# Two-layer transformer kernel: where the conformer convolution and its layer norm stand in the second block

## The chip, the cores and the metric

One core of a Trainium2 chip (trn2) runs the whole kernel in one launch. The metric is device time in microseconds (us) of one execution, lower is better. The core has TensorE (PE in the profile; its weight loads are PEld), VectorE (DVE), ScalarE (ACT), GpSimd (POOL), and SyncE (SP), which here issues every DMA.

## The reference

A first block (`first_block`: a gated short convolution, a latent attention, a retention) gives `x`, 512 tokens by 1024. It isn't touched by the change. The second block follows, and all is f32:

```python
def conformer_conv(a, b, dw_w, dw_b, ln_g, ln_b):
    u = a * jax.nn.sigmoid(b)
    ...
    u = lax.conv_general_dilated(u, dw_w[:, None, :], window_strides=(1,), ...,   # 31 taps, depthwise
                                 feature_group_count=C) + dw_b
    u = layer_norm(u, ln_g, ln_b)
    return jax.nn.silu(u)

def second_block(x, ...):
    h = rms_norm_2(x, norm1_g)
    z = jnp.einsum('bsd,dc->bsc', h, w_in)
    q, k = rope(rms_norm_2(heads(z[q]), ...)), rope(rms_norm_2(heads(z[k]), ...))   # 8 heads of 64
    attn = ...                     # three dilated windows, mixed by their log-sum-exp
    conv = conformer_conv(z[a], z[b], ...)                                          # 512 channels
    x = x + jnp.einsum('bsc,cd->bsd', jnp.concatenate([attn, conv]), w_out)
    x = x + expert_choice_moe(rms_norm_2(x, norm2_g), w_router, w1, w3, w2)         # 16 experts, 64 tokens each
```

(`...` and `z[...]` shorten it.) The experts' weights are 16 times 33.8 MB.

## The kernel before

The engines are programmed by hand, each with its own instruction stream in program order; named semaphores tie them together. A wait blocks all that stands behind it on the same engine. `PS[:, b, :]` are the 8 banks of the accumulator memory (PSUM), 128 x 512 f32 each.

The part of the second block that matters here runs in these stages. Feature-major means that channels lie on partitions and the 512 tokens on columns; token-major is the other way round.

1. **Gated input** (`f2_psum`): four groups j of 128 channels of a and b, feature-major, are projected; sigmoid and product give `CU2` (`cu_done`). SyncE then copies `CU2` into shifted copies `RG` (`spread(b)`, 16 DMAs for each b, semaphore `rg_in[b]`), from which the convolution of 128 channels is 32 matmuls in the program (64 in the trace) with the diagonal weights `DWD[b]` that GpSimd builds (`dwd_ready`).
2. **q/k/v loop**, i = 0 to 11: TensorE projects tile t = i % 4 of 128 tokens for q (i < 4), k (i < 8) and v into bank 4 + i % 4 (`z_psum`). For q and k ScalarE squares it and takes a seed of the root (Ln, Exp), VectorE reduces, refines, scales and rotates (`zr_ready`), and TensorE transposes the result in `turn_z(i - 1)`, one projection later. `conv(b)` stands behind projections 1, 3, 5 and 7. ScalarE moves its result to `CA[:, b, :]` (`conv_out`, `cv_done`).
3. **Second attention**, n = 0 to 15 (token tile n // 4, pair of heads n % 4): TensorE makes two score matmuls (`scores2`), VectorE masks them and finds the row maxima (`row_max2`), ScalarE exponentiates (`probs2`), VectorE divides (`norm_p2`), TensorE transposes the 2 x 4 blocks (`turn_p2`), ScalarE copies them out (`pt2_out`), TensorE multiplies by v (`values2`), and after each token tile ScalarE copies the outputs (`yt2_out`, `yt2_evac`).
4. **Layer norm over channels**, spread over the pairs n = 0 to 7 of stage 3 (`LN_AT = 0`): the mean by four matmuls with `LN_ONES` (n = 0), four subtractions on VectorE (`cen_done`) and four squares on ScalarE (`lsq_done`, n = 1), the variance by four matmuls (n = 2), the inverse root (ScalarE's Ln and Exp, then three passes on VectorE), for each group j a scaling and an affine pass (`ly_ready`, n = 3 to 6), ScalarE's Exp(-y) (`ly_exp`), and VectorE's `silu`: add 1, reciprocal, multiply (`y2_done`, n = 4 to 7).
5. **Output projection** `out_project2` with the router between its parts, then top-k on VectorE, then the experts. The expert weights go through a ring of 12 slots of 1.4 MB. SyncE issues the first ten loads once `yt2_evac` is 4 and `y2_done` is 4, two more when the output projection is through, and each later one when TensorE has used the slot (`ring_used`).

What sets the order around the change is thus code order on each engine. SyncE's queue around stage 2 holds, in this order: `spread(0)`, `spread(1)`, the weights of k (group 11, needed at i = 4), `spread(2)`, `spread(3)`, the weights of v (group 12, released by `z_psum` 4), then those of the output projection (13 and 14, released by `z_psum` 8 and 12), then the expert loads.

Of the kernel before, what the change touches and what calls it, by code (L numbers as in the profile page):

```python
# [28 lines left out]
ALU = mybir.AluOpType  # L29
# [109 lines left out]
def build(nc, x, meta, wd, w_uq, w_ukv, w_router, w1, w3, w2, prm, ident_d, tab_d, iota_d, mask_d, out):  # L139
    with ExitStack() as ctx:  # L140
# [146 lines left out]
        pt_evac ptm_evac ps_ready pv_psum yo_free op_psum xo_done ustat2 u2_ready ut2_psum ut2_ready  # L287
        pads dwd_ready conv_psum f2_psum b_exp cu_done z_psum z_sq z_ms z_rs z_free zr_ready zT_psum zT_evac v_evac s2_psum nm2_ready
        p2_done pt2_psum pt2_evA pv2_psum ps2_ready yt2_evac cv_done mean_psum cen_done lsq_done
        var_psum lv_ready lrs_done ly_ready ly_exp y2_done op2_psum xo2_done rstat h2n_ready h2T_psum h2T_ready lg_psum  # L290
# [113 lines left out]
        def _(gp):  # L404
# [35 lines left out]
            for b in range(4):  # L440
                if b == 2:
                    gp.wait_ge(s["ut2_psum"], NT)
# [5 lines left out]
        def _(act):  # L448
# [137 lines left out]
            for t in range(NT):  # L586
                act.wait_ge(s["xo_done"], 2 * t + 2)
                if t >= 2:
                    act.wait_ge(s["ut2_psum"], t - 1)
                own(act.activation(U2[t % 2], X[:, t, :], ACT.Square, accum_out=stat[:, t:t + 1]))  # L590
                own.settle()
                rsqrt_seed(rstd[:, t:t + 1], stat[:, t:t + 1], 1.0 / D).then_inc(s["ustat2"], 1)
# [20 lines left out]
            for i in range(2 * NT):  # L613
# [32 lines left out]
            for n in range(NT * 4):  # L646
# [5 lines left out]
                if n == LN_AT + 1:  # L652
                    for j in range(4):
                        act.wait_ge(s["cen_done"], j + 1)
                        act.activation(LSQ[:, j, :], CA[:, j, :], ACT.Square).then_inc(s["lsq_done"], 1)
                if n == LN_AT + 2:
                    act.wait_ge(s["lv_ready"], 1)
                    own(act.activation(LY, LV, ACT.Ln))
                    own.settle()
                    act.activation(LY, LY, ACT.Exp, scale=-0.5).then_inc(s["lrs_done"], 1)  # L660
                if n >= LN_AT + 3 and n < LN_AT + 7:
                    j = n - LN_AT - 3
                    act.wait_ge(s["ly_ready"], j + 1)
                    if j >= 2:
                        act.wait_ge(s["y2_done"], j - 1)
                    act.activation(SCB[j % 2], CA[:, j, :], ACT.Exp, scale=-1.0).then_inc(s["ly_exp"], 1)
# [4 lines left out]
            for t in range(NT):  # L671
# [3 lines left out]
                rsqrt_seed(rstd[:, t:t + 1], stat[:, t:t + 1], 1.0 / D).then_inc(s["rstat"], 1)  # L675
# [31 lines left out]
        def _(dve):  # L707
# [283 lines left out]
            def norm_row(t):  # L991
                dve.wait_ge(s["ustat2"], t + 1)
                refine(rstd[:, t:t + 1], stat[:, t:t + 1], 1.0 / D)
                dve.tensor_scalar(U2[t % 2], X[:, t, :], rstd[:, t:t + 1], None, ALU.mult).then_inc(s["u2_ready"], 1)

            def rowT_out(t):
                c = t * P
                dve.wait_ge(s["ut2_psum"], t + 1)
# [4 lines left out]
                i.then_inc(s["ut2_ready"], 1)  # L1003
# [10 lines left out]
            for j in range(4):  # L1014
                dve.wait_ge(s["b_exp"], j + 1)
                dve.wait_ge(s["f2_psum"], 2 * j + 2)
                silu(SCB[j % 2], PS[:, (2 * j + 1) % 4, :], CU2[:, j, PAD:PAD + S]).then_inc(s["cu_done"], 1)

            for i in range(2 * NT):
# [21 lines left out]
                dve.tensor_tensor(t1, t1, t2, ALU.add).then_inc(s["zr_ready"], 1)  # L1041

# [22 lines left out]
            for n in range(NT * 4):  # L1065
# [784 lines left out]
```

## Time and profile before

| | |
|---|---|
| median of 3 runs | 2061.91 us (2059.35 to 2061.99) |
| the profiled execution | 2061.4 us, its span 2059.6 us |
| TensorE busy | 1828.9 us, 89% of the span |
| VectorE, ScalarE busy | 477.2 us (23%), 206.9 us (10%) |
| DMA queue q1 | 70.3% of 16 engines' span, 597.93 MB |
| chain that ended last | DMA 48%, PE 39%, SPq 5%, DVE 4%, ACT 2% |

The busy shares are means over stages with different limits, so they don't tell what one stage is worth. The chain tells which work the end waited for at each moment. An idle time on an engine is named with what ended it. The time outside of the span (2061.4 - 2059.6 = 1.8 us) is no part of any view.

### The profile page before, as it was taken

To read this page: it belongs to the slowest core of one execution; us is meant where nothing else is said; L and a number is where in the kernel's file an instruction comes from. 1 tells how busy PE (TensorE), PEld (TensorE's weight loads), DVE (VectorE), ACT (ScalarE), POOL (GpSimd) and SP (SyncE) were. 2 spreads that over 40 slices of the span, in tenths; PEclk is the share of its full clock that TensorE was granted. 3 is DMA by queue.
4 is the path that set the end of the run, shared out by engine and by line. 5 is a ranking of instruction groups with operands and counts; after the bars stand their busy time and mean duration, and the time that the engine had idled before them with its cause. 6 is when DMAs were issued, how large, how long until landed. Compare 5 with 4: busy or idle time off the path is not lost.

```text
span 2059.6 us, 20333 instructions
## 1 busy us (share of the span) xinstructions
PE 1828.9 (89%) x8256; PEld 771.3 (37%) x8256; DVE 477.2 (23%) x965; ACT 206.9 (10%) x413; POOL 15.0 (1%) x30
## 2 busy tenths in 40 slices
PE   7998999989997969998888988988988889889887
PEld 4544446444344533333332332332323323323222
DVE  2453336224328240120110101201201111012011
ACT  2131014000124210000000000000000000000000
POOL 0000000100000000000000000000000000000000
PEclk9899799999997989999999999999999999999999
DMA  6102020034210617999999999999999999999998
GB/s 239 47 0 82 0 82 1 24 116 110 82 42 1 263 75 329 424 424 426 425 426 425 426 426 426 425 426 426 426 426 426 426 425 426 426 426 426 426 425 347
DMA packets 82035, 598.53 MB, mean 291 GB/s; under 512 B 8824, under 2 KB 18168, under 8 KB 32712
## 3 DMA queue, kind: packets, MB, share of 16 engines
q1 hardware_dynamic: 81992, 597.93, 70.3%
q8 instruction: 30, 0.49, 0.1%
q14 instruction: 13, 0.11, 0.0%
HBM read 591.38 MB, written 2.10 MB: 288 GB/s over the span
## 4 chain that ended last, share of the span: by engine, by line
DMA 48%; PE 39%; SPq 5%; DVE 4%; ACT 2%; issue 1%; DVEq 0%; ACTq 0%
DMA arena<-in_w 48%; PE PS L1217 19%; PE PS L1687 5%; SPq L391 5%; PE PS L1601 3%; PE PS L1720 2%; PE PS L1517 1%; PE PS L1340 1%; PE PS L1400 1%; DVE arena L789 1%; PE PS L1270 1%; PE PS L1657 1%; PE PS L1430 1%; PE PS L1414 1%; PE PS L1562 1%
## 5 line engine op out<-in xcount | busy, mean ns | idle before, releaser
L1687 PE MATMUL PS<-arena 128*64 128x512 f32 (+1 forms) x3072 | 639.7, 562 | 112.5 <-DMA arena<-in_w 111.7
L1687 PEld LDWEIGHTS PS<-arena 128*64 128x64 f32 x3072 | 207.6, 136 | 544.9 <-issue 354.8
L1217 PE MATMUL PS<-arena 128*128 128x512 f32 (+6 forms) x1040 | 391.4, 535 | 3.2 <-DVE arena L1000 1.4
L1720 PE MATMUL PS<-arena 128*64 128x512 f32 x1408 | 324.5, 599 | 23.5 <-ACT arena L698 13.1
L1217 PEld LDWEIGHTS PS<-arena 128*128 128x128 f32 (+1 forms) x1040 | 186.0, 194 | 197.5 <-issue 188.6
L1720 PEld LDWEIGHTS PS<-arena 128*64 128x64 f32 x1408 | 115.5, 137 | 222.5 <-issue 168.1
L1182 DVE TENSOR_TENSOR arena<-arena,PS 128x1408 f32<-128x1408 f32 x16 | 25.9, 1621 | 699.0 <-PE PS L1687 699.0
L694 ACT ACTIVATE arena<-PS 128x1408 f32<-128x1408 f32 x16 | 21.5, 1344 | 742.7 <-PE PS L1687 742.7
L1191 DVE COPY arena<-PS 128x512 f32<-128x512 f32 x16 | 11.1, 692 | 328.3 <-PE PS L1720 328.3
L1734 PE MATMUL PS<-arena 64*128 64x512 f32 x256 | 76.7, 626 | 8.9 <-DVE arena L1176 8.1
L1199 DVE TENSOR_TENSOR arena<-arena,PS 128x512 f32<-128x512 f32 x128 | 78.0, 682 | 20.4 <-PE PS L1734 20.4
L1657 PE MATMUL PS<-arena 128*64 128x512 f32 x256 | 59.4, 607 | 1.5 <-DVE arena L1163 1.5
L1601 PE MATMUL PS<-arena 128*128 128x512 f32 x128 | 57.3, 595 | 0.7 <-ACT arena L643 0.7
L789 DVE RECIPROCAL arena<-arena 128x512 f32<-128x512 f32 x16 | 53.6, 3353 | 0.6
L688 ACT ACTIVATE arena<-PS 128x512 f32<-128x512 f32 x16 | 9.6, 598 | 438.6 <-PE PS L1657 438.6
L1734 PEld LDWEIGHTS PS<-arena 64*128 64x128 f32 x256 | 31.1, 185 | 43.4 <-DVE arena L1199 26.0
L1562 PE MATMUL PS<-arena 128*64 128x128 f32 x256 | 19.8, 303 | 16.2 <-ACT arena L639 13.5
L1601 PEld LDWEIGHTS PS<-arena 128*128 128x128 f32 x128 | 23.3, 190 | 26.0 <-issue 25.1
L1657 PEld LDWEIGHTS PS<-arena 128*64 128x64 f32 x256 | 18.8, 140 | 35.5 <-issue 35.5
L787 DVE TENSOR_SCALAR arena<-arena 128x512 f32<-128x512 f32 x16 | 6.8, 426 | 97.6 <-PE PS L1217 44.5
L1707 PEld LDWEIGHTS PS<-arena 128*128 128x128 f32 x176 | 23.0, 213 | 14.6 <-issue 12.2
L1517 PE MATMUL PS<-arena 128*32 128x512 f32 x256 | 28.3, 594 | 0.0
(242 smaller groups left out, 974.3 us busy)
## 6 DMA issues: line engine op xcount, KB each, us to landing
arena<-in_w SPq DMA_DIRECT2D x384, 1408.0 KB, 34.6
arena<-in_w_in SPq DMA_DIRECT2D x5, 2048.0 KB, 7.8
arena<-in_w_in SPq DMA_DIRECT2D x8, 1024.0 KB, 6.4
arena<-in_w_out SPq DMA_DIRECT2D x4, 2048.0 KB, 8.4
arena<-arena SPq DMA_DIRECT2D x64, 67.5 KB, 2.3
arena<-in_tab SPq DMA_DIRECT2D x1, 2304.0 KB
arena<-in_w_in SPq DMA_DIRECT2D x1, 2176.0 KB, 19.2
arena<-in_x SPq DMA_DIRECT2D x4, 512.0 KB, 6.6
```

Source lines behind the costliest of these rows:

```text
L391: sp.dma_start(RING[n % SLOTS], chunk(e, n)).then_inc(ring_in[n % SLOTS], 16)
L789: own(dve.reciprocal(e, e))
L1182: dve.tensor_tensor(HH, S1, PF[:, 3 * 512:3 * 512 + FH], ALU.mult).then_inc(s["hh_done"], 1)
L1199: dve.tensor_tensor(xs, xs, PS[:, [3, 4, 5, 7][n % 4], :], ALU.add).then_inc(s["sc_add"], 1)
L1217: i = pe.matmul(dst, lhs(k), rhs(k), start=k == 0, stop=k == KD - 1)
L1517: ins = pe.matmul(PS[CG_W * i:CG_W * (i + 1), 2 + b % 2, :], DWD[b][:, n * CG_W:(n + 1) * CG_W], RG[4 * b + i][:, SH * q:SH * q + S], star ...
L1562: ins = pe.matmul(PS[64 * f:64 * f + 64, 6, j * P:(j + 1) * P], V2[:, b * 512 + h * HD:b * 512 + (h + 1) * HD], PT2[:, f, b * P:(b + 1) * ...
L1601: ins = pe.matmul(PS[:, i % 4, :], YT2[:, k, t * P:(t + 1) * P], wg[:, k, :], start=k == 0, stop=k == KD - 1)
L1657: i = pe.matmul(PS[64 * f:64 * f + 64, 7, :], SEL[:, t, :], H2N[:, t, f * 512:(f + 1) * 512], start=t == 0, stop=t == NT - 1, skip_group_c ...
L1687: i = pe.matmul(PS[64 * f:64 * f + 64, bank + c // 512, 0:w], XE[:, k, :], slot[:, f * FH + c:f * FH + c + w], start=k == 0, stop=k == KD ...
L1720: ins = pe.matmul(PS[64 * d:64 * d + 64, 6, :], HT[:, j, 64 * f:64 * f + 64], W2R[:, f, j, d * 512:(d + 1) * 512], start=f == 0 and j == 0 ...
L1734: pe.matmul(PS[:, [3, 4, 5, 7][n % 4], :], G[64 * d:64 * d + 64, t * P:(t + 1) * P], YE[64 * d:64 * d + 64, :], start=True, stop=True).the ...
```

## The change

The computation stays. `conv(b)` stands behind projections 0, 1, 2 and 3. The mean's matmuls stand behind projection 4 and use bank 2 in place of bank 7, the variance's behind projection 5 in bank 3. The rest of the layer norm follows on ScalarE and VectorE in the q/k iterations 4 to 6 and behind iteration 7. The sigmoid in it is taken in another way: in place of VectorE's add, reciprocal and multiply, VectorE adds 1 (and caps at 1e18), ScalarE takes Ln and Exp(-x), VectorE multiplies. Stage 3 keeps nothing but the attention. Some semaphores are merged into others with an offset (`ut2_psum` into `ut_psum` from 5 on, and the like), at the same points of the program.

```diff
 ACT, q/k loop
-                if i >= 3 and i % 2 == 1:
-                    conv_out((i - 3) // 2)
-            zT_out(2 * NT - 1)
-            conv_out(3)
-            for t in range(NT):
+                if i < 4:
+                    conv_out(i)
+                if i == 4:
+                    for j in range(4):
+                        act.wait_ge(s["cen_done"], j + 1)
+                        act.activation(LSQ[:, j, :], CA[:, j, :], ACT.Square).then_inc(s["lsq_done"], 1)
+                if i == 5:
+                    act.wait_ge(s["lv_ready"], 1)
+                    own(act.activation(LY, LV, ACT.Ln))
+                    own.settle()
+                    act.activation(LY, LY, ACT.Exp, scale=-0.5).then_inc(s["lrs_done"], 1)
+
+            def ln_exp(j):
+                act.wait_ge(s["ly_ready"], j + 1)
+                if j >= 2:
+                    act.wait_ge(s["y2_done"], j - 1)
+                act.activation(SCB[j % 2], CA[:, j, :], ACT.Exp, scale=-1.0).then_inc(s["ly_exp"], 1)
+
+            def ln_sig(j):
+                act.wait_ge(s["ly_one"], j + 1)
+                own(act.activation(SCB[j % 2], SCB[j % 2], ACT.Ln))
+                own.settle()
+                act.activation(SCB[j % 2], SCB[j % 2], ACT.Exp, scale=-1.0).then_inc(s["ly_sig"], 1)
+            ln_exp(0), ln_exp(1), ln_sig(0), ln_sig(1)
+            zT_out(2 * NT - 1)
+            ln_exp(2), v_out(0), ln_exp(3), ln_sig(2), ln_sig(3)
+            for t in range(1, NT):
+                v_out(t)
 DVE, behind the rotation of q/k iteration i
+                if i == 4:
+                    dve.wait_ge(s["mean_psum"], 1)
+                    dve.wait_ge(s["cv_done"], 4)
+                    for j in range(4):
+                        dve.tensor_tensor(CA[:, j, :], CA[:, j, :], PS[:, 2, :], ALU.subtract).then_inc(s["cen_done"], 1)
+                if i == 5:
+                    dve.wait_ge(s["var_psum"], 1)
+                    dve.tensor_scalar(LV, PS[:, 3, :], EPS, None, ALU.add).then_inc(s["lv_ready"], 1)
+                if i == 6:
+                    dve.wait_ge(s["lrs_done"], 1)
...
+                    ln_affine(0), ln_affine(1)
+            ln_one(0), ln_affine(2), ln_one(1), ln_out(0), ln_affine(3), ln_out(1)
+            ln_one(2), ln_one(3), ln_out(2), ln_out(3)
 DVE, second attention: the same passes and silu leave pairs 1 to 7
-                if LN_AT + 4 <= n < LN_AT + 8:
-                    j = n - LN_AT - 4
-                    dve.wait_ge(s["ly_exp"], j + 1)
-                    silu(SCB[j % 2], CA[:, j, :], YT2[:, 4 + j, :]).then_inc(s["y2_done"], 1)
 PE, q/k loop
-                if i < 2 * NT and i % 2 == 1:
-                    conv(i // 2)
+                if i < 4:
+                    conv(i)
+                if i == 4:
+                    pe.wait_ge(s["cv_done"], 4)
+                    for j in range(4):
+                        ins = pe.matmul(PS[:, 2, :], LN_ONES, CA[:, j, :], start=j == 0, stop=j == 3)
+                    ins.then_inc(s["mean_psum"], 1)
+                if i == 5:
+                    pe.wait_ge(s["cen_done"], 4)
+                    pe.wait_ge(s["lsq_done"], 4)
+                    for j in range(4):
+                        ins = pe.matmul(PS[:, 3, :], LN_ONES, LSQ[:, j, :], start=j == 0, stop=j == 3)
+                    ins.then_inc(s["var_psum"], 1)
```

`ln_affine(j)` is the scaling by LY and the affine pass of group j, `ln_one(j)` the cap and add, `ln_out(j)` the last multiply. The order of the instructions on TensorE in the q/k/v loop before (L1217 is a projection of 8 matmuls, its x80 is the gated input's 64 and projections 0 and 1; L1503 is `turn_z`, L1517 a convolution):

```order
L1217 MATMUL PS<-arena 128x512 x80
L1503 MATMUL PS<-arena 128x128 x4
L1517 MATMUL PS<-arena 32x512 x32
L1217 MATMUL PS<-arena 128x512 x8
L1503 MATMUL PS<-arena 128x128 x4
L1217 MATMUL PS<-arena 128x512 x8
L1503 MATMUL PS<-arena 128x128 x4
L1517 MATMUL PS<-arena 32x512 x32
L1217 MATMUL PS<-arena 128x512 x8
L1503 MATMUL PS<-arena 128x128 x4
```

After, from projection 2 on (L1237 a projection, L1523 `turn_z`, L1537 a convolution, L1556 the mean's matmuls, L1562 the variance's):

```order
L1237 MATMUL PS<-arena 128x512 x8
L1523 MATMUL PS<-arena 128x128 x4
L1537 MATMUL PS<-arena 32x512 x32
L1237 MATMUL PS<-arena 128x512 x8
L1523 MATMUL PS<-arena 128x128 x4
L1537 MATMUL PS<-arena 32x512 x32
L1237 MATMUL PS<-arena 128x512 x8
L1523 MATMUL PS<-arena 128x128 x4
L1556 MATMUL PS<-arena 128x512 x4
L1237 MATMUL PS<-arena 128x512 x8
L1523 MATMUL PS<-arena 128x128 x4
L1562 MATMUL PS<-arena 128x512 x4
```

The four convolutions stand within the first four iterations, and the mean and the variance behind projections 4 and 5. On VectorE, pair n = 4 of the second attention before (L1090 and L1092 the scaling and the affine pass, L787 to L791 `silu`, L1057 and L1061 `norm_p2`, L1050 `row_max2`):

```order
L1057 RECIPROCAL arena<-arena 128x2
L1061 TENSOR_SCALAR arena<-arena 128x512 x2
L1050 ISA arena<-PS,arena 128x512
L1050 ISA arena 128x1
L1050 ISA arena<-PS,arena 128x512
L1050 ISA arena 128x1
L1090 TENSOR_TENSOR arena<-arena 128x512
L1092 TENSOR_SCALAR arena<-arena 128x512
L787 TENSOR_SCALAR arena<-arena 128x512
L789 RECIPROCAL arena<-arena 128x512
L791 TENSOR_TENSOR arena<-arena 128x512
```

After, VectorE from the end of q/k iteration 6 to the start of iteration 7 (L1068 ends the rotation, L1080 to L1084 finish the inverse root, L1033 and L1035 are `ln_affine`, L1052 is iteration 7's reduction):

```order
L1068 TENSOR_TENSOR arena<-arena 128x512
L1080 TENSOR_TENSOR arena<-arena 128x512
L1082 SCALAR_TENSOR_TENSOR arena<-arena 128x512
L1084 SCALAR_TENSOR_TENSOR arena<-arena 128x512
L1033 TENSOR_TENSOR arena<-arena 128x512
L1035 TENSOR_SCALAR arena<-arena 128x512
L1033 TENSOR_TENSOR arena<-arena 128x512
L1035 TENSOR_SCALAR arena<-arena 128x512
L1052 TENSOR_REDUCE arena<-arena 128x8
```

and behind iteration 7 (L1039 `ln_one`, L1044 `ln_out`):

```order
L1066 TENSOR_TENSOR arena<-arena 128x8x32
L1068 TENSOR_TENSOR arena<-arena 128x512
L1039 TENSOR_SCALAR arena<-arena 128x512
L1033 TENSOR_TENSOR arena<-arena 128x512
L1035 TENSOR_SCALAR arena<-arena 128x512
L1039 TENSOR_SCALAR arena<-arena 128x512
L1044 TENSOR_TENSOR arena<-arena 128x512
L1033 TENSOR_TENSOR arena<-arena 128x512
L1035 TENSOR_SCALAR arena<-arena 128x512
L1044 TENSOR_TENSOR arena<-arena 128x512
L1039 TENSOR_SCALAR arena<-arena 128x512 x2
L1044 TENSOR_TENSOR arena<-arena 128x512 x2
```

The layer norm's passes left the pairs; seven of them now stand ahead of iteration 7's reduction, and the sigmoid's passes behind its rotation, with no reciprocal among them.

## Rows read from the trace of the kernel before

**Rows 1.** the page, section 2 (40 equal slices of 51.5 us) and section 4 (chain by engine):
```profile
DMA  6102020034210617999999999999999999999998
...
DMA 48%; PE 39%; SPq 5%; DVE 4%; ACT 2%; issue 1%; DVEq 0%; ACTq 0%
```

**Rows 2.** the chain that ended last, in order of time: start us, us, what:
```profile
494.23 7.00 PE PS L1517 x64
501.23 7.06 PE PS L1217 x16
...
516.04 7.00 PE PS L1517 x64
...
595.54 1.15 PE PS L1541 x4
...
687.54 10.57 PE PS L1601 x24
...
779.85 19.11 PE PS L1687 x96
...
908.32 33.68 DMA arena<-in_w
```

**Rows 3.** timeline of SyncE's DMA queue: start us, us of issuing, line, what:
```profile
480.55 21.57 SPq L357 DMA_DIRECT2D arena<-arena  x32
...
559.25 35.91 SPq L330 DMA_DIRECT2D arena<-in_w_out  x2
687.52 64.72 SPq L391 DMA_DIRECT2D arena<-in_w  x12
```

**Rows 4.** timeline of VectorE in the second attention: head pairs 0, 1, 9 and 15:
```profile
598.96 0.17 DVE L1057 RECIPROCAL arena<-arena 128x2 f32<-128x2 f32 x1 [0.98 <-ACT arena L632]
...
602.24 0.17 DVE L1057 RECIPROCAL arena<-arena 128x2 f32<-128x2 f32 x1 [0.98 <-ACT arena L632]
...
660.49 0.17 DVE L1057 RECIPROCAL arena<-arena 128x2 f32<-128x2 f32 x1 [0.98 <-ACT arena L632]
...
680.67 0.17 DVE L1057 RECIPROCAL arena<-arena 128x2 f32<-128x2 f32 x1 [1.02 <-ACT arena L632]
```

**Rows 5.** groups by line, 595 to 688 us: line engine op count | busy, mean ns | idle before:
```profile
L789 DVE RECIPROCAL arena<-arena 128x512 f32<-128x512 f32 x4 | 13.4, 3353 | 0.1
...
L1578 PE MATMUL PS<-arena 128*128 128x512 f32 x8 | 3.6, 592 | 0.0
...
L1090 DVE TENSOR_TENSOR arena<-arena 128x512 f32<-128x512 f32 x4 | 2.8, 689 | 0.0
...
L666 ACT ACTIVATE arena<-arena 128x512 f32<-128x512 f32 x4 | 2.5, 630 | 16.8 <-DVE arena L1092 16.8
L1074 DVE TENSOR_TENSOR arena<-arena,PS 128x512 f32<-128x512 f32 x4 | 2.5, 682 | 0.1
...
L1092 DVE TENSOR_SCALAR arena<-arena 128x512 f32<-128x512 f32 x4 | 2.2, 546 | 0.1
```

**Rows 6.** stretches of the second attention: busy us and instructions per engine, PEclk, DMA share, GB/s:
```profile
595.00:612.00 17.00, 13.63 (x83) 7.30 (x84) 10.59 (x29) 9.09 (x19) 0.00 (x0) 1.00 0.34 125
628.00:650.00 22.00, 15.38 (x92) 9.48 (x94) 21.61 (x34) 9.32 (x19) 0.00 (x0) 0.68 0.00 1
662.00:688.00 26.00, 21.16 (x201) 14.90 (x202) 13.18 (x42) 16.94 (x33) 0.00 (x0) 0.98 0.01 2
```

**Rows 7.** timeline of ScalarE, projections 0 and 4 of q/k/v:
```profile
486.96 0.60 ACT L617 ACTIVATE arena<-PS 128x512 f32<-128x512 f32 x1 [13.14 <-PE PS L1217]
...
530.14 0.60 ACT L617 ACTIVATE arena<-PS 128x512 f32<-128x512 f32 x1 [11.55 <-PE PS L1217]
```

**Rows 8.** timeline of VectorE, first and last instruction on projection 0:
```profile
487.59 0.69 DVE L1025 TENSOR_REDUCE arena<-arena 128x8 f32<-128x512 f32 x1 [2.89 <-ACT arena L617]
...
491.69 0.69 DVE L1041 TENSOR_TENSOR arena<-arena 128x512 f32<-128x512 f32 x1
```

**Rows 9.** timeline of TensorE, one value product at the lower clock:
```profile
620.16 1.97 PE L1562 MATMUL PS<-arena 128*64 128x128 f32 x16 [3.36 <-ACT arena L639]
```

More of the change, by code:

```diff
@@ L651, in _ @@
                     yt2_out(n // 4 - 1)
[L652 to L666, printed above, removed]
             pt2_out(NT * 4 - 1)
@@ L1017, in _, with ln_affine, ln_one, ln_out @@
                 silu(SCB[j % 2], PS[:, (2 * j + 1) % 4, :], CU2[:, j, PAD:PAD + S]).then_inc(s["cu_done"], 1)
+            def ln_affine(j):
+                dve.wait_ge(s["cen_done"], 4)
+                dve.wait_ge(s["lsq_done"], 4)
+                own(dve.tensor_tensor(CA[:, j, :], CA[:, j, :], LY, ALU.mult))
+                own.settle()
+                dve.tensor_scalar(CA[:, j, :], CA[:, j, :], prm_c("lng", j), prm_c("lnb", j), ALU.mult, ALU.add).then_inc(s["ly_ready"], 1)
+            def ln_one(j):
+                dve.wait_ge(s["ly_exp"], j + 1)
+                dve.tensor_scalar(SCB[j % 2], SCB[j % 2], 1.0e18, 1.0, ALU.min, ALU.add).then_inc(s["ly_one"], 1)
+            def ln_out(j):
+                dve.wait_ge(s["ly_sig"], j + 1)
+                dve.wait_ge(s["ly_ready"], j + 1)
+                dve.tensor_tensor(YT2[:, 4 + j, :], SCB[j % 2], CA[:, j, :], ALU.mult).then_inc(s["y2_done"], 1)
             for i in range(2 * NT):
@@ L1041, in _ @@
                 dve.tensor_tensor(t1, t1, t2, ALU.add).then_inc(s["zr_ready"], 1)
+                if i == 4:
[8 more added lines that the diff above has]
+                    dve.wait_ge(s["lrs_done"], 1)
+                    dve.wait_ge(s["lv_ready"], 1)
+                    own(dve.tensor_tensor(LA, LY, LY, ALU.mult))
+                    own.settle()
+                    own(dve.scalar_tensor_tensor(LA, LA, -0.5, LV, ALU.mult, ALU.mult))
+                    own.settle()
+                    own(dve.scalar_tensor_tensor(LY, LA, 1.5, LY, ALU.add, ALU.mult))
+                    own.settle()
+                    ln_affine(0), ln_affine(1)
+            ln_one(0), ln_affine(2), ln_one(1), ln_out(0), ln_affine(3), ln_out(1)
+            ln_one(2), ln_one(3), ln_out(2), ln_out(3)
             def row_max2(i):
@@ L1480, in _ @@
             turn_row(NT - 1)
-            pe.wait_ge(s["ut2_ready"], NT)
+            pe.wait_ge(s["ut_ready"], 5 + NT)
             pe.wait_ge(s["xo_done"], 2 * NT)
@@ L1567, in _ @@
             pe.wait_ge(s["v_evac"], NT)
+            pe.wait_ge(s["lv_ready"], 1)
             scores2(0), scores2(1)
@@ L1574, in _ @@
                 turn_p2(n)
-                if n == LN_AT:
-                    pe.wait_ge(s["cv_done"], 4)
-                    for j in range(4):
-                        ins = pe.matmul(PS[:, 7, :], LN_ONES, CA[:, j, :], start=j == 0, stop=j == 3)
-                    ins.then_inc(s["mean_psum"], 1)
-                if n == LN_AT + 2:
-                    pe.wait_ge(s["cen_done"], 4)
-                    pe.wait_ge(s["lsq_done"], 4)
-                    for j in range(4):
-                        ins = pe.matmul(PS[:, 7, :], LN_ONES, LSQ[:, j, :], start=j == 0, stop=j == 3)
-                    ins.then_inc(s["var_psum"], 1)
             values2(NT * 4 - 1)
```

55 lines of the change are left out of this document (15 added, 40 removed).

## The prediction

> **What bounds the kernel now.** I read the page's slices first. The DMA row stands at 9 in 23 slices from the seventeenth on, that is from some 824 us, and the chain by engine gives DMA 48% of the span [rows 1]. A reader could stop there: the kernel is bound by the expert weights, and an attention ahead of them would be worth nothing. So the question is what starts that stream. The chain in order of time answers it [rows 2]: it is TensorE's all through the q/k/v loop (494 us), the second attention (595.54), the output projection (687.54) and the first expert (779.85), and DMA comes into it only at 908.32. And SyncE's queue shows the expert loads beginning at 687.52, within 0.1 us of the output projection [rows 3]; they wait for the last `yt2_out`, and the later ones for slots that TensorE frees. The stream therefore hangs on the same event as the compute. If the second attention ends earlier, the loads, the top-k and all 16 experts start earlier by as much.
>
> So two stretches matter: the q/k/v loop, and the second attention from 595.54 to 687.54, 92.0 us [rows 2]. The attention is a relay, VectorE to ScalarE to TensorE and back. Left alone, a pair of heads takes 602.24 - 598.96 = 3.28 us on VectorE, as between pairs 0 and 1. Pairs 9 to 15, where the layer norm is over, take 680.67 - 660.49 = 20.18 us for six steps, 3.36 each, the copies of two token tiles (after pairs 9 and 13) within [rows 4]. Pairs 1 to 9 take 660.49 - 602.24 = 58.25 us for eight steps, 7.28 each [rows 4]. In these stand the four reciprocals of 3.35 us and some 24 other passes of the layer norm on VectorE, and ScalarE and TensorE wait for it [rows 5]: in 628 to 650 VectorE is busy 21.61 of 22 us, TensorE 15.38, while in 662 to 688 it is 13.18 of 26 against 21.16 [rows 6].
>
> **The change, part by part.** *The convolutions.* They keep their number and stand earlier. Behind four projections in place of eight, they leave the sum of the loop as it was: TensorE is in the chain without a gap there, a convolution 7.00 us, two projections 7.06 each, two transposes 0.35 each, 21.81 us from one convolution to the next [rows 2]. What could hold an earlier convolution is its data. Projection 0 ends at 486.96 and projection 4 at 530.14, where ScalarE takes them up [rows 7]. `spread(2)` and `spread(3)` are issued from 480.55 over 21.57 us, so until 502.1 [rows 3]. In the changed order conv(1) begins behind projection 1, one convolution and one projection after 486.96, at 501; conv(2) one cycle of 14.4 us later, at 515.8, and conv(3) at 530. Their last copies are issued at 491 and 502, so there is a cover of 24 and 28 us. Copies 0 and 1 stand ahead of 480.55 in the queue. The wait for v's weights (`z_psum` 4) comes at 530 in place of 516 and they are wanted 50 us later. Cost 0; without the cover, each us of lateness would be one.
>
> *The mean and the variance.* 2 x 8 matmuls of the trace at 3.53 us per eight (half a projection of 7.06; in the attention eight take 3.6) [rows 2, 5] now stand in a stretch where TensorE never waits: +7.1 us on the path.
>
> *The layer norm's waits in the loop.* Projection 4 ends two convolutions later, T4 = 530.14 + 14.1 = 544.2. VectorE needs 5.4 us from the end of a projection to the end of its rotation (486.96 to 491.69 + 0.69) [rows 7, 8]. Hence the centring begins at T4 + 5.4 and is done at T4 + 7.9 (four in 2.5 us), the squares one ACTIVATE of 0.63 later, T4 + 8.6 [rows 5]. TensorE gets to the variance after transpose, mean, projection 5 and transpose: 0.35 + 3.5 + 7.06 + 0.35 = T4 + 11.3. The cover is 2.7 us, cost 0. Projection 5 ends at T5 = T4 + 11.0 and projection 6 at T6 = T5 + 11.0; the inverse root's Ln and Exp stand on ScalarE at T5 + 6.1 to 7.4, with nothing needed from it before T6. In iteration 6 VectorE adds three passes at 0.69 and two of (0.69 + 0.55), 4.6 us [rows 5], and is free at T6 + 10.0. Iteration 7's reduction, due at T6 + 7.4 + 0.6, starts 2.0 us late, and its rotation, 4.8 us later, is ready at T6 + 14.8. TensorE asks for it (transpose 7, behind projection 8) at T6 + 2 x 7.4 = 14.8. So this just about touches: I take 0.3 us, between 0 and 2.0 (all of the lateness). Behind it stand only the v projections; the rest of the norm, some 10 us on ScalarE and VectorE from T6 + 14.8, runs under three of them (21 us), and `v_out(0)` to `v_out(2)` among it are not what the scores wait for. Cost 0.
>
> *The second attention without it.* It starts 7.1 + 0.3 later, at 602.9. From its first scores to pair 0 on VectorE 598.96 - 595.54 = 3.4 us. Steps 0 to 9: nine at 3.28 and one tile's copy in them, (20.18 - 6 x 3.28) / 2 = 0.25, so 29.8 us. Steps 9 to 15: 20.2. From pair 15 to the output projection 687.54 - 680.67 = 6.9 us [rows 2, 4]. Sum 60.3 us, against 92.0: -31.7. The tail may be shorter, since TensorE had arrears there: 5.5 at the least, which gives -33.1. At the other end, all steps at 3.36 and a tile's copy once more in full give 61.3, thus -30.7.
>
> *The rest.* The output projection's second weights, issued at 595.2 (559.25 + 35.91) [rows 3] behind `z_psum` 12, move to 602 and are wanted at 663. Its wait for `y2_done` is over at some 591. The sum is -31.7 + 7.1 + 0.3 = -24.3 us on the profiled execution's 2061.4 (span and 1.8 around it), **2037.1 us**, 1.2% less; the median of the runs is 0.5 above that execution. The two ends of the costs are -33.1 + 7.1 = -26.0 and -30.7 + 7.2 + 2.0 = -21.5, or 2035.4 to 2039.9.
>
> *The clock, where a rule speaks against this.* The attention without the norm is nothing but short bursts of matmuls with a wait in each step. In 662 to 688, which is that pattern and no other, the granted clock was 0.98, and 1.00 in 595 to 612; it fell to 0.68 in 628 to 650, where TensorE waited for the reciprocals [rows 6]. The Trainium skill, "TensorE: Matmul & The Clock Gate", section "A second HAM failure mode: psum-queue depth-cycling", says that small idle times between groups of matmuls, from cycling through PSUM in each iteration, are enough to make the clock oscillate between its two levels. By that rule the stretch that gets longer here would be slow; by the rows it is the stretch that was fast, and the cause of the low clock leaves. I go by the rows, and the rule is rival A.
>
> **The rivals.** *A, the clock stays at its lower level (1.2 GHz) in the attention; slower than before.* A value product of 16 then takes 1.97 us, as at 620.16 [rows 9], and the transposes and the scores, I take it, as much: 5.9 us of TensorE per pair, which is more than VectorE's 3.28. Sixteen pairs make 94.5 and some 6 of tail, 100 us: +8.5 + 7.4 = +16, **2077 us**. It decides from the tenth slow pair on (24.3 us over 5.9 - 3.28 = 2.6). For it: a clock of 0.68 stood in this very stage. Against it: 0.98 in the same pattern, and that at the lower clock TensorE would have no waits at all. 2%; a few slow pairs, up to 2045, 4%.
>
> *B, the norm's chain isn't covered in the loop.* If TensorE waited for all of it: centring and squares 3.1, variance, Ln and Exp 2.0, iteration 6's passes 4.6, thus 9.7 us and **2046.8**. For it: in one place the margin is nil. Against it: the others are over 2.5 us, and VectorE works 4.8 us on a q/k projection [rows 8] where the loop gives it 10.9 on the average (21.81 for two) [rows 2]. 6%, with parts of it.
>
> *C, the stream of weights hides it.* If the loads were set by the memory from their first on, the earlier compute would find them late and the end would move by nothing, **2061 to 2069**. Against it, as above, 687.52 and 908.32 [rows 2, 3]. 2%. That the change doesn't do what it says would be this time too; the order of instructions speaks against it.
>
> *D, a gain of more than 26 us,* through a shorter relay than pairs 9 to 15 show: 3%.
>
> **How the numbers follow.** The forecast, 2035 to 2040, has 83%. The range takes in D's near part and the parts of B: 2033 to 2042. What a measurement can tell here is about 0.2%, 4 us, either way. Faster by more than that: the forecast, B and the few slow pairs of A, D, 95%; no change: C in part, 2%; slower: A in full and C with the loop's 7 us, 3%.
>
> **What would show each step.** In the profile after: the q/k/v loop ends, and the scores begin, at 602 to 603.5, TensorE without a gap but at transpose 7; eight matmuls twice in it at 3.5 us. The attention takes 59 to 61.5 us, its pairs 3.3 to 3.4 on VectorE from first to last, the clock at 0.95 or more in it, and no reciprocal of 3.35 us after 490. The expert loads begin at some 663, and the chain turns to DMA at 884. A clock of 0.7 in the attention would be A; a wait of TensorE for VectorE or ScalarE in iterations 4 to 8 above 2 us would be B; loads that land late for the first expert would be C.

## The result, and the profile after

The changed kernel takes 2038.2 us (median of 4 runs, 2035.5 to 2038.6), the kernel before beside it 2061.7 (4 runs, 2059.4 to 2062.0): ratio 0.9888, 95% interval 0.9876 to 0.9900, so 1.1% faster. The forecast was 2037.1, within a range of 2033 to 2042. The profiled execution took 2035.54 us, with a span of 2033.8; it was the shortest of the four, and the other three lie at 2038.2 to 2038.6.

The page first: the DMA row of the 40 slices, and the chain by engine (compare [rows 1]).

```profile
DMA  6101020034120629999999999999999999999998
...
DMA 49%; PE 39%; SPq 6%; DVE 3%; ACT 2%; issue 1%; DVEq 0%; ACTq 0%
```

Little in them has changed. The chain in order of time (start us, us, what) shows what did; it answers to [rows 2]:

```profile
542.98 3.44 PE PS L1556 x8
...
553.72 3.44 PE PS L1562 x8
...
600.77 1.15 PE PS L1572 x4
...
660.59 10.57 PE PS L1620 x24
...
753.46 19.11 PE PS L1706 x96
...
881.92 33.69 DMA arena<-in_w
```

The scores begin at 600.77 instead of 595.54, and the output projection at 660.59 instead of 687.54: the attention is 59.82 us long instead of 92.00. From there on all is as before, 27 us earlier: the first expert at 753.46 (92.87 us behind the projection; before 92.31), the chain's turn to DMA at 881.92. L1556 and L1562 are the mean and the variance, 3.44 us each, in the path now. SyncE's queue (start us, us of issuing, line, what; compare [rows 3]) hands out the expert weights at the same moment as the output projection begins:

```profile
660.57 131.88 SPq L391 DMA_DIRECT2D arena<-in_w  x28
```

VectorE at pairs 0, 1 and 15 of the second attention (L1104 is `norm_p2`'s short reciprocal; compare [rows 4]):

```profile
604.19 0.17 DVE L1104 RECIPROCAL arena<-arena 128x2 f32<-128x2 f32 x1 [0.98 <-ACT arena L658]
...
607.47 0.17 DVE L1104 RECIPROCAL arena<-arena 128x2 f32<-128x2 f32 x1 [0.98 <-ACT arena L658]
...
653.72 0.17 DVE L1104 RECIPROCAL arena<-arena 128x2 f32<-128x2 f32 x1 [1.02 <-ACT arena L658]
```

The steps are all 3.28 us but the last two (3.58 and 3.32). Three stretches of it (busy us and instructions of each engine, then PEclk, DMA share, GB/s; compare [rows 6]):

```profile
603.00:620.00 17.00, 14.65 (x123) 9.09 (x124) 11.54 (x37) 11.84 (x27) 0.00 (x0) 1.00 0.25 96
620.00:640.00 20.00, 18.46 (x165) 11.52 (x164) 13.60 (x42) 16.36 (x33) 0.00 (x0) 1.00 0.01 2
640.00:664.00 24.00, 19.22 (x164) 12.67 (x164) 10.12 (x31) 13.28 (x26) 0.00 (x0) 1.00 0.11 38
```

(The last stretch reaches 3.4 us into the output projection.) The granted clock is 1.00 in all three, where it was 0.68 in the middle before. The loop, on TensorE at its tightest place, `turn_z(7)` behind projection 8:

```profile
571.60 7.03 PE L1237 MATMUL PS<-arena 128*128 128x512 f32 x16
578.78 0.65 PE L1523 MATMUL PS<-arena 128*128 128x128 f32 x4
579.27 20.77 PE L1237 MATMUL PS<-arena 128*128 128x512 f32 x48
```

Projection 8 would hand over at 571.60 + 6.87 = 578.47; the transposes begin at 578.78, a wait of 0.31 us. On VectorE the cause and its end (L1073 the centring, L1052 the reduction of iteration 7, L1044 the norm's last multiply):

```profile
547.92 2.47 DVE L1073 TENSOR_TENSOR arena<-arena,PS 128x512 f32<-128x512 f32 x4
...
573.94 0.68 DVE L1052 TENSOR_REDUCE arena<-arena 128x8 f32<-128x512 f32 x1
...
586.31 0.69 DVE L1044 TENSOR_TENSOR arena<-arena 128x512 f32<-128x512 f32 x1 [0.49 <-ACT arena L644]
```

Projection 6 ended at 563.86, so the reduction was due 8.0 later at 571.9 by the prediction's working; it starts at 573.94, behind the affine passes; the norm is over at 587.0, 13.8 us ahead of the scores.

### The profile page after: what moved, and what is told of

It is laid out like the page before. It is cut to its first block, busy times and chain, and to the rows that moved or that the text cites. A ratio compares the mean times of both kernels' runs of the same rounds, so it can differ in the third digit from the quotient of the medians.

```text
span 2033.8 us, 20341 instructions
## 1 busy us (share of the span) xinstructions
PE 1817.5 (89%) x8256; PEld 764.8 (38%) x8256; DVE 463.6 (23%) x961; ACT 212.8 (10%) x421; POOL 15.1 (1%) x30
## 4 chain that ended last, share of the span: by engine, by line
DMA 49%; PE 39%; SPq 6%; DVE 3%; ACT 2%; issue 1%; DVEq 0%; ACTq 0%
DMA arena<-in_w 48%; PE PS L1237 18%; PE PS L1706 6%; SPq L391 5%; PE PS L1620 3%; PE PS L1739 2%; PE PS L1537 1%; PE PS L1360 1%; PE PS L1420 1%; PE PS L1593 1%; PE PS L1676 1%; ACT arena L665 1%; PE PS L1450 1%; PE PS L1581 1%; PE PS L1434 1%
## 5 line engine op out<-in xcount | busy, mean ns | idle before, releaser
L1237 PE MATMUL PS<-arena 128*128 128x512 f32 (+6 forms) x1040 | 395.8, 540 | 3.2 <-DVE arena L1011 1.4
L1237 PEld LDWEIGHTS PS<-arena 128*128 128x128 f32 (+1 forms) x1040 | 188.8, 198 | 199.3 <-issue 190.5
L1202 DVE TENSOR_TENSOR arena<-arena,PS 128x1408 f32<-128x1408 f32 x16 | 25.9, 1621 | 699.2 <-PE PS L1706 699.2
L800 DVE RECIPROCAL arena<-arena 128x512 f32<-128x512 f32 x12 | 40.2, 3353 | 0.4
L1537 PE MATMUL PS<-arena 128*32 128x512 f32 x256 | 28.3, 594 | 0.0
L1207 DVE COPY arena<-PS 128x896 f32<-128x896 f32 x16 | 17.5, 1092 | 44.5 <-PE PS L1726 44.5
```

The costliest lines, as they stand in the source:

```text
L800: own(dve.reciprocal(e, e))
L1202: dve.tensor_tensor(HH, S1, PF[:, 3 * 512:3 * 512 + FH], ALU.mult).then_inc(s["hh_done"], 1)
L1237: i = pe.matmul(dst, lhs(k), rhs(k), start=k == 0, stop=k == KD - 1)
L1537: ins = pe.matmul(PS[CG_W * i:CG_W * (i + 1), 2 + b % 2, :], DWD[b][:, n * CG_W:(n + 1) * CG_W], RG[4 * b + i][:, SH * q:SH * q + S], star ...
```

## The experiments

One table for all of them, from the profiled execution of each: T0 is the end of projection 0, where ScalarE takes it up; then the loop (T0 to the first scores), the attention (to the output projection), the way to the first expert, and the rest of the span. The last columns are the median of its runs and the ratio to runs of the kernel before that were made beside it; the medians of these were 2061.7 beside the changed kernel and 2061.1 or 2061.2 beside the others.

| kernel | T0 | loop | attention | to expert | rest | median | ratio (95%) |
|---|---|---|---|---|---|---|---|
| before | 486.96 | 108.58 | 92.00 | 92.31 | 1279.75 | 2061.7 | 1 |
| changed | 485.00 | 115.77 | 59.82 | 92.87 | 1280.34 | 2038.2 | 0.9888 (0.9876, 0.9900) |
| e1 | 486.57 | 115.76 | 59.82 | 92.80 | 1279.95 | 2037.4 | 0.9884 (0.9867, 0.9900) |
| e2 | 485.55 | 108.58 | 89.32 | 93.61 | 1279.74 | 2060.2 | 0.9993 (0.9984, 1.0003) |
| e3 | 487.20 | 108.59 | 91.99 | 92.31 | 1280.21 | 2062.1 | 1.0005 (0.9996, 1.0014) |
| e4 | 487.38 | 108.58 | 59.83 | 92.99 | 1279.82 | 2030.0 | 0.9846 (0.9829, 0.9862) |
| e5 | 488.03 | 108.59 | 59.82 | 93.04 | 1280.32 | 2030.0 | 0.9842 (0.9826, 0.9859) |
| e6 | 487.98 | 115.78 | 68.03 | 92.23 | 1279.98 | 2042.3 | 0.9910 (0.9895, 0.9925) |
| e7 | 486.68 | 115.77 | 59.83 | 95.32 | 1280.10 | 2038.1 | 0.9892 (0.9877, 0.9907) |
| e8 | 486.74 | 122.86 | 59.83 | 95.31 | 1280.16 | 2044.5 | 0.9923 (0.9909, 0.9936) |
| e9 | 486.96 | 108.58 | 75.30 | 92.12 | 1280.14 | 2045.0 | 0.9924 (0.9907, 0.9940) |
| e10 | 488.59 | 108.59 | 87.79 | 95.32 | 1279.51 | 2061.2 | 0.9999 (0.9989, 1.0009) |
| e11 | 482.98 | 112.27 | 59.82 | 93.64 | 1280.19 | 2032.7 | 0.9868 (0.9851, 0.9884) |
| e12 | 485.01 | 110.26 | 59.82 | 92.28 | 1279.83 | 2030.7 | 0.9856 (0.9840, 0.9873) |

**e1: the changed kernel with `silu` as it was.** The sigmoid is VectorE's add, reciprocal and multiply again, in the new place.

```diff
-            ln_exp(0), ln_exp(1), ln_sig(0), ln_sig(1)
+            ln_exp(0), ln_exp(1)
             zT_out(2 * NT - 1)
-            ln_exp(2), v_out(0), ln_exp(3), ln_sig(2), ln_sig(3)
+            v_out(0), ln_exp(2), ln_exp(3)
...
-            ln_one(0), ln_affine(2), ln_one(1), ln_out(0), ln_affine(3), ln_out(1)
-            ln_one(2), ln_one(3), ln_out(2), ln_out(3)
+            ln_affine(2), ln_affine(3)
+            ln_silu(0), ln_silu(1), ln_silu(2), ln_silu(3)
```

> The changed kernel with the sigmoid of the layer norm taken as before (VectorE adds 1, takes the reciprocal, multiplies) in place of Ln and Exp on ScalarE; the place of everything stays. If the gain comes from where the layer norm stands, this costs nothing: behind iteration 7's rotation (578.6 us) VectorE has 2 affine pairs of 1.2 and four times 4.5 us, done by some 599.5, and the first row maximum is wanted at 601.9. 2038 us, equal to the changed kernel within 1 us. If the gain needs the reciprocals gone, it loses 13 us or so: 2051.

Loop and attention are those of the changed kernel to 0.01 us. VectorE has its four long reciprocals under the v projections, where it has nothing else:

```profile
583.03 3.35 DVE L794 RECIPROCAL arena<-arena 128x512 f32<-128x512 f32 x1
...
596.38 3.35 DVE L794 RECIPROCAL arena<-arena 128x512 f32<-128x512 f32 x1
```

The last ends at 599.73 and the scores begin at 602.33. The new sigmoid is worth nothing in this place.

**e2: the kernel before, with the new sigmoid alone.** Ln and Exp(-x) on ScalarE one pair behind Exp(-y), the multiply on VectorE one pair later.

```diff
+                if n >= LN_AT + 4 and n < LN_AT + 8:
+                    j = n - LN_AT - 4
+                    act.wait_ge(s["ly_one"], j + 1)
+                    own(act.activation(SCB[j % 2], SCB[j % 2], ACT.Ln))
+                    own.settle()
+                    act.activation(SCB[j % 2], SCB[j % 2], ACT.Exp, scale=-1.0).then_inc(s["ly_sig"], 1)
...
-                    silu(SCB[j % 2], CA[:, j, :], YT2[:, 4 + j, :]).then_inc(s["y2_done"], 1)
+                    dve.tensor_scalar(SCB[j % 2], SCB[j % 2], 1.0e18, 1.0, ALU.min, ALU.add).then_inc(s["ly_one"], 1)
```

> The kernel before, with only the sigmoid changed: the layer norm stays in pairs 0 to 8 of the second attention, VectorE adds 1, ScalarE takes Ln and Exp, VectorE multiplies one pair later. Pairs 4 to 7 took 7.85 us each; VectorE then works 2.3 + 1.2 + 0.4 + 0.7 = 4.6 us in a pair and ScalarE 2.8 + 0.6 + 1.3 = 4.7, in a relay, so 5.5 us: 4 x 2.3 = 9 us less, 2052.5. If the removal of the reciprocals were the whole gain: 2038. If the two engines only swap the work within the relay: 2060.

13.4 us of reciprocals are gone from VectorE, and the attention is 2.7 us shorter where 9 were expected. The median is 0.9 us lower, which is no clear difference, though its interval still holds 2.7 us. Pair 6 shows why so little came of it, first on VectorE, then on ScalarE:

```profile
643.88 0.68 DVE L1107 TENSOR_TENSOR arena<-arena 128x512 f32<-128x512 f32 x1
647.90 0.17 DVE L1063 RECIPROCAL arena<-arena 128x2 f32<-128x2 f32 x1 [3.35 <-ACT arena L632]
```

```profile
644.65 0.63 ACT L666 ACTIVATE arena<-arena 128x512 f32<-128x512 f32 x1 [3.65 <-DVE arena L1107]
645.19 0.61 ACT L670 ACTIVATE arena<-arena 128x512 f32<-128x512 f32 x1
645.83 0.63 ACT L672 ACTIVATE arena<-arena 128x512 f32<-128x512 f32 x1
646.37 0.70 ACT L632 ACTIVATE arena<-arena 128x512 f32<-128x512 f32 x1
```

VectorE ends its passes at 644.56 and then waits 3.35 us. ScalarE had waited 3.65 us until that moment, since its Exp(-y) (L666) stands ahead of the next probabilities (L632) and needs the affine pass and the buffer that the multiply (L1107) frees, which VectorE comes to only behind the row maxima of the next pair. When ScalarE runs, VectorE has nothing, and the reverse. The two take turns, and a step is 7.77 us: 4.4 of VectorE and 3.35 of ScalarE. The lower clock isn't the cause: it is 0.73 in 628 to 650, but from 614.4 to 648.8 the chain that ended last runs over VectorE and ScalarE alone, without TensorE.

**e3: the kernel before, with the convolutions early alone.**

```diff
-                if i < 2 * NT and i % 2 == 1:
-                    conv(i // 2)
+                if i < 4:
+                    conv(i)
```

> The kernel before, with only the convolutions moved behind projections 0 to 3. Prediction: cost 0, since the copies of the input are there 24 us and more ahead: 2061.7, and the second attention starts at the same time. If the earlier convolutions waited for their data or for cv_done: slower by the wait, some us.

The loop takes 108.59 against 108.58: the move costs nothing, and brings nothing by itself.

**e4 and e5: both kernels without the layer norm.** The channel layer norm and its silu are left out, and ScalarE copies the convolutions' output to YT2 behind `v_out(0)`.

In e4:

```diff
+                if t == 0:
+                    act.wait_ge(s["cv_done"], 4)
+                    for j in range(4):
+                        act.activation(YT2[:, 4 + j, :], CA[:, j, :], ACT.Copy).then_inc(s["y2_done"], 1)
```

> The kernel before without the channel layer norm and its silu (no mean, no variance, no sigmoid; ScalarE copies the convolution's result to YT2 behind v's first copy instead, under the v projections). It prices all that the layer norm cost in the second attention. By the prediction's terms the attention falls from 92.0 to 60 us: 2061.7 - 32 = 2029.7. If another thing than the layer norm held the early pairs back, less than 25 us.

> The changed kernel without the channel layer norm and its silu, in the same way. It prices what the layer norm costs where it stands now: 16 matmuls of the trace, 6.9 us, and 0.3 us of TensorE's wait for the transpose of iteration 7. 2038.2 - 7.2 = 2031, within 1.5 us of the kernel before without the norm. If the moved norm were for free: 2038. If it costs more than the matmuls: below 2029.

Both leave out a part of the computation and serve as a price only. Both come to 2030.0 us. The norm costs 92.00 - 59.83 = 32.2 us in the old place and 115.77 - 108.59 = 7.2 in the new one; of the 7.2, 6.88 are its matmuls and 0.31 the wait at `turn_z(7)`. By the medians it is 31.2 (against the kernel before beside e4) and 8.2.

**e6: four reciprocals put back into the attention of the changed kernel,** of data that nobody reads.

```diff
                     row_max2(2 * n + 2), row_max2(2 * n + 3)
+                if 4 <= n < 8:
+                    own.settle()
+                    own(dve.reciprocal(LA, LV))
```

> The changed kernel with one more 128x512 reciprocal on VectorE (of LV into the unused LA) in each of the pairs 4 to 7 of the second attention. Theory 1, the relay alone: VectorE's step becomes 2.3 + 3.4 = 5.7 us in place of 3.28, four times +2.4 = +10 us, 2048, and the granted clock in these pairs stays near 1. Theory 2, TensorE's waits also pull its clock down: a granted clock under 0.8 in the stretch, TensorE's bursts at 1.97 us in place of 1.09, and more than 12 us: 2050 to 2055.

VectorE at one of the four, and the stretch with all of them:

```profile
622.52 3.35 DVE L1118 RECIPROCAL arena<-arena 128x512 f32<-128x512 f32 x1
625.78 0.11 DVE L1104 RECIPROCAL arena<-arena 128x2 f32<-128x2 f32 x1
```

```profile
615.00:635.00 20.00, 15.83 (x138) 9.75 (x134) 17.90 (x35) 12.31 (x26) 0.00 (x0) 1.00 0.00 1
```

The four steps take 5.48, 5.43, 5.43 and 5.43 in place of 3.28, and the attention is 8.2 us longer: VectorE is the bound in these steps, with 17.90 of 20 us busy, and a step is the reciprocal (3.26 from start to start) and 2.2 us of the relay's own passes. The clock stays at 1.00, so a reciprocal in the relay does not by itself bring it down. So theory 1 of the expectation holds in its mechanism, with 8.2 us for its 10, and theory 2 does not. The runs scatter (2040.0 to 2045.8), and their median is only 4.1 us over the changed kernel's, not the 8.2 of the attention. The profiled execution is the slowest of the four, with a T0 3.0 us later than the changed kernel's; what made the others shorter was not seen.

**e7: the expert loads held back in the changed kernel.**

```diff
             sp.wait_ge(s["y2_done"], 4)
+            sp.wait_ge(s["op2_psum"], 4)
```

> The changed kernel with the first ten expert loads held until half of the output projection is through (some 693 us in place of 660.6). The prediction has the stream hang on the compute: the ten slots take 34 us and are wanted at 753, so 33 us of lateness at the start costs nothing, 2038. If the start of the stream is what the end waits for (DMA at its limit from there on): +33 us, 2071.

SyncE's queue, and the chain at the output projection, the first expert and the turn to DMA:

```profile
694.90 101.68 SPq L392 DMA_DIRECT2D arena<-in_w  x28
```

```profile
662.28 12.26 PE PS L1621 x24
...
757.60 19.11 PE PS L1707 x96
...
886.06 33.95 DMA arena<-in_w
```

The loads begin at 694.90, 34 us later than in the changed kernel (1.7 of it since all of this execution is later, as its T0 shows), and from the first expert to the turn is 886.06 - 757.60 = 128.46 us, as there (881.92 - 753.46). The medians are the same. So at least with a start up to some 33 us later, it is the first expert's compute that the stream of weights follows, not its own start.

**e8: the variance directly behind the mean,** so that nothing covers the centring and the squares.

```diff
                     ins.then_inc(s["mean_psum"], 1)
-                if i == 5:
                     pe.wait_ge(s["cen_done"], 4)
```

> The changed kernel with the variance's matmuls directly behind the mean's, in iteration 4, so that projection 5 no longer covers the centring and the squares. TensorE then waits from T4 + 3.8 us to T4 + 8.6: +4.8 us, 2043, and a wait of that size for ScalarE shows in the profile. If the order doesn't matter since other waits shrink: 2038.

TensorE's groups in 545 to 565 us (busy us, mean ns, idle before), and the granted clock:

```profile
L1561 PE MATMUL PS<-arena 128*128 128x512 f32 x8 | 5.7, 883 | 4.8 <-ACT arena L627 4.8
L1556 PE MATMUL PS<-arena 128*128 128x512 f32 x8 | 3.6, 592 | 0.0
```

```profile
535.00:548.00 13.00, 13.00 (x52) 5.28 (x43) 2.54 (x8) 2.28 (x5) 0.00 (x0) 1.00 0.15 56
...
553.00:559.00 6.00, 6.00 (x10) 2.56 (x11) 0.00 (x0) 0.00 (x0) 0.00 (x0) 0.66 0.01 3
559.00:575.00 16.00, 16.00 (x45) 7.54 (x44) 5.48 (x14) 4.14 (x10) 0.00 (x0) 1.00 0.00 0
```

The wait is 4.8 us, as expected, but the loop is 7.1 longer. The eight matmuls behind the wait take 5.7 us where the same ones take 3.6, at a granted clock of 0.66: 4.8 + 2.1 = 6.9. The expectation had the wait and not the clock behind it, and its 2043 came out as 2044.5.

**e9: e2 with every step of the norm a pair behind the one that feeds it.**

```diff
-                if n >= LN_AT + 3 and n < LN_AT + 7:
-                    j = n - LN_AT - 3
+                if n >= LN_AT + 4 and n < LN_AT + 12 and (n - LN_AT) % 2 == 0:
+                    j = (n - LN_AT - 4) // 2
```

(and in the same manner the add, Ln with Exp, and the multiply at n = 5 + 2j, 6 + 2j and 7 + 2j)

> The kernel before with Ln and Exp for the sigmoid (as in e2_lnexp_only), and with each of its steps placed a pair of heads or more behind the step that feeds it, and ahead of nothing that it holds up: ScalarE's Exp(-y) of group j at pair 4 + 2j, VectorE's add at 5 + 2j, Ln and Exp at 6 + 2j, the multiply at 7 + 2j. The mean and the variance stay in pairs 0 to 3. Theory from e2_lnexp_only: what made pairs 4 to 7 take 7.8 us each was not the reciprocal but that ScalarE's Exp stood ahead of the next probabilities and waited for VectorE's passes behind the row maxima, so that the two engines took turns. With the waits gone the pairs from 4 on take 3.6 to 4.1 us: 12 us less, 2048.5. If it is the sheer amount of work on the two engines: as e2_lnexp_only, 2060.

The same instructions as e2 in the same stage, and the attention is 75.30 us in place of 89.32. All engines are busy at once:

```profile
622.00:664.00 42.00, 35.93 (x310) 23.20 (x309) 34.64 (x96) 35.01 (x71) 0.00 (x0) 0.96 0.01 1
```

ScalarE 35.01 and VectorE 34.64 of 42 us; no step from pair 4 on is over 4.6 us. By the medians this is 16.1 us less than the kernel before beside it (12 were expected), some seven tenths of what the change brings, without a move into the loop.

What e9 leaves is the part of the norm that it didn't touch. Its steps from pair 1 to 4 still take 7.01, 9.98 and 5.58 us, 12.7 us over three undisturbed ones, of the 15.5 by which its attention is longer than the changed kernel's. The first two are as long in the kernel before, and neither has a long reciprocal or the sigmoid in it. There the chain runs through the mean, the squares and the variance, with TensorE's matmuls (from the chain of the kernel before):

```profile
601.20 3.45 PE PS L1578 x8
...
605.39 1.82 ACT arena L655 x3
...
612.30 3.45 PE PS L1584 x8
```

No run takes these steps apart; the change takes them out of the attention with the rest.

**e10: the kernel before, Exp(-y) and `silu` each a pair later, reciprocals kept.**

```diff
-                if n >= LN_AT + 3 and n < LN_AT + 7:
-                    j = n - LN_AT - 3
+                if n >= LN_AT + 4 and n < LN_AT + 8:
+                    j = n - LN_AT - 4
```

> The kernel before with its reciprocals, only Exp(-y) and silu placed one pair later, so that ScalarE doesn't wait for VectorE ahead of the probabilities. VectorE then has 2.3 + 1.2 + 4.5 = 8 us of work in a pair of which 3.4 is the reciprocal, and is the bound by itself: 2061, no gain. So the reciprocal and the wait each suffice to hold the pairs at 7.8 us. If the wait alone was the cause: 2050.

The attention of the profiled execution is 4.2 us shorter, yet the medians are equal, and the interval leaves out 4.2 (more on this at the end). VectorE is now bound by its own work:

```profile
624.00:640.00 16.00, 12.15 (x90) 7.85 (x89) 15.65 (x33) 8.84 (x18) 0.00 (x0) 0.82 0.00 1
640.00:660.00 20.00, 14.21 (x80) 8.03 (x79) 19.65 (x29) 7.82 (x17) 0.00 (x0) 0.72 0.00 1
```

Its four steps with a reciprocal take 7.85, 7.85, 6.66 and 6.67 us. So either is enough to hold a step at 6.7 to 7.9 us: the turns that the engines take (e2), or VectorE's own work with a long reciprocal in it (e10). Only e9, without both, gets away.

**e11: the changed kernel with the groups summed on VectorE first,** and one matmul each for mean and variance.

```diff
+                if i == 2:
+                    dve.wait_ge(s["cv_done"], 2)
+                    own(dve.tensor_tensor(LA, CA[:, 0, :], CA[:, 1, :], ALU.add))
...
-                    for j in range(4):
-                        ins = pe.matmul(PS[:, 3, :], LN_ONES, LSQ[:, j, :], start=j == 0, stop=j == 3)
+                    ins = pe.matmul(PS[:, 3, :], LN_ONES, LY, start=True, stop=True)
```

> The changed kernel, where VectorE adds up the four groups of channels (the convolution's results in iterations 2 and 3, the squares in iteration 4) and TensorE takes one matmul over the sum in place of four, for the mean and for the variance. TensorE's part falls from 6.9 to 1.7 us in the loop where it never waits; the variance's cover gets shorter by 2.6 us for the mean and VectorE's last add comes 0.7 us later, so a wait of 0.8 us may appear. 2038.2 - 5.2 + 0.8 = 2033.8, better than both kernels. If the loop is bound by another engine: 2038.

The loop is 3.5 us shorter. It would be 5.2 (six matmuls fewer at 0.86; the trace counts each as two), but the sum of the squares is late: the transposes ahead of the variance begin at 548.53 and would hand over 0.43 later, the variance begins at 550.50 and holds the engine 0.96 instead of 0.86. That is 1.6 us where 0.8 was expected, and 5.2 - 1.6 = 3.6 is close to the 3.5 measured.

**e12: e11 with the variance a projection later,** behind projection 6, the inverse root behind iteration 7, and `zT_out(7)` ahead of `ln_exp(0)`.

```diff
-                if i == 5:
+                if i == 6:
                     pe.wait_ge(s["cen_done"], 6)
```

> As e11_groups_summed_first, with the variance behind projection 6 in place of 5 and the inverse root and first affine passes behind iteration 7's rotation in place of 6's. The 0.8 us of wait ahead of the variance and the 0.3 us ahead of transpose 7 go: 1.1 us less than e11_groups_summed_first, 2032.7, and no wait of TensorE in the loop. The rest of the norm ends some 7 us later, at about 592, still ahead of the scores. If it doesn't fit: scores or output projection late by some us.

TensorE in the loop (L1571 the mean, L1575 the variance, L1539 `turn_z`, L1253 projections):

```profile
542.83 1.02 PE L1571 MATMUL PS<-arena 128*128 128x512 f32 x2
543.69 7.03 PE L1253 MATMUL PS<-arena 128*128 128x512 f32 x16
...
558.30 1.02 PE L1575 MATMUL PS<-arena 128*128 128x512 f32 x2
...
573.34 0.60 PE L1539 MATMUL PS<-arena 128*128 128x128 f32 x4
573.77 20.77 PE L1253 MATMUL PS<-arena 128*128 128x512 f32 x48
```

No wait is left: 110.26 us against 108.58 without a norm, 1.7 us, which are the two matmuls, and 2.0 less than in e11, where 1.1 were expected. Against the changed kernel that is 5.5: the six matmuls and the 0.31 at `turn_z(7)`. The median is 2030.7, the lowest of all the kernels that compute the whole: 30.4 us below the kernel before beside it and 7.5 below the changed kernel. The loop explains 5.5 of the 7.5, and the other 2.0 are within what executions of one kernel differ by.

## Why the prediction was right

It was right in its mechanism and nearly in each term. By its own steps:

- *The stream of weights hangs on the attention's end.* Shown. Expert loads, first expert and turn to DMA came 27, 26.4 and 26.4 us earlier, and e7 shows a later start of the loads to cost nothing. Rival C falls.
- *The convolutions move at no cost.* Shown by e3: 0.01 us.
- *Mean and variance +7.1.* They took 6.88.
- *The wait at `turn_z(7)` 0.3, the other waits none.* 0.31; the reduction started 2.0 us late, as worked out. e8 is rival B's mechanism made real, and shows that the cover is needed: the variance's data came 4.8 us behind the mean's matmuls, and a projection and four transposes, 7.3 us, stood there in the change.
- *The attention 60.3 us.* It took 59.82, and e4 and e5 have the same without any norm. The steps are 3.28 but for the last two (3.58 and 3.32), where the sum had 3.28 for nine and 3.36 for six, and 0.25 for a copy of a token tile: the copies behind the earlier tiles made no step longer.
- *The clock.* It was 1.00 in all three stretches of the attention, so rival A falls. In the kernel before, the low clock was no term of the attention's length either: from 616 to 661 us the chain runs over VectorE and ScalarE alone. The Trainium skill, "TensorE: Matmul & The Clock Gate", section "A second HAM failure mode: psum-queue depth-cycling", says that small idle times between groups of matmuls, from cycling through PSUM in each iteration, make the clock oscillate between its two levels. Such idle times are here all along the stage, with PE busy 14.65 of 17 us and 19.22 of 24; here the trace does not agree with the page. In the kernel before, where it did fall to its lower level at times, TensorE's longest wait was 3.36 us [rows 9]; what the fall needs is not shown here.
- *The sum.* Loop and attention changed by +7.19 - 32.18 = -25.0, against -24.3. The profiled execution is 25.9 us shorter, since its T0 was 2.0 us earlier and the two stretches behind the attention 1.2 longer; the medians differ by 23.5. The prediction, made for the profiled execution, lies 1.6 above that and 1.1 below the median. That it came so near either is in part luck, as executions of one kernel differ by more.

What was read too shortly is the cause of the long steps, 7.28 us on the average. The text has ScalarE and TensorE waiting for VectorE with its four reciprocals. But e1 shows that the gain doesn't need the reciprocals gone, and e2 that their going is not enough: without them the old attention is 2.7 us shorter. The second cause was in the rows already, in L666's 16.8 us of waiting for the affine pass [rows 5]: ScalarE's Exp(-y) stood one step too near to what feeds it. And the average hid a third: step by step, pairs 1 to 9 take 7.01, 9.98, 7.77, 7.86, 7.85, 7.84, 6.67 and 3.27 us. The first two, 10.4 of the 32 us too long, are the waits around mean and variance. The number wasn't hurt, as the whole norm left the stage; a forecast for e2 made from the reciprocals alone, 4 x 3.35 us, would have missed by 10.7.

That the early convolutions make the gain possible is argued, not measured by itself: the mean needs all four of them, and before the change the last of them stood behind the last q/k projection.

## What to carry to other kernels

A side chain that shares engines with a relay costs by its place in the program order more than by its work: put each of its steps a turn behind the one that feeds it (e2 to e9: the same instructions, 14 us less), or better, under an engine that is busy without a gap (the change: 32 us for 7). Ahead of a stream that takes 48% of the chain, ask what starts the compute that it follows; an earlier stage can be worth its full length. And once a side chain lies in a stretch that one engine bounds, that engine's share is all that is left to save, and passes on an idle engine buy it (e12: two matmuls for eight, -5.5 us).

## What the runs showed of the hardware

After a wait of 4.8 us TensorE ran its next eight matmuls at a granted clock of 0.66 and gave away 2.1 us more (e8), while the attention's waits of a few tenths to one us in each step left it at 1.00 (the changed kernel).

Executions of one kernel differ by 1 to 7 us (e9's four by 1.2, the thirteen of the kernel before beside it by 7.1), and two places show a part of it. The output projection's first 24 matmuls take 10.57 us in the changed kernel and 12.26 in e7 (above), with a granted clock in that place of 1.00 and 0.87; the gather's 16 take 6.02 and 6.67. Together these are 2.34 of the 2.45 us by which the stretch to the first expert is longer in e7. The other place is ahead of the change: T0 lies between 483.0 and 488.6 in the table, in code that all the kernels share. What makes either place shorter or longer stays open. In e10's profiled execution a T0 1.6 us later and 3.0 us in this stretch cancel the attention's 4.2; whether its other runs have the same reasons for their unmoved median was not seen.
